# Norm gains applied at the transposes' eviction, a fifth slot for split weights, constants first, wider pauses in the compressed branch

## The reference

```python
def rms_norm(x, gain):
    y = x * lax.rsqrt(jnp.mean(x * x, axis=-1, keepdims=True) + NORM_EPS)
    return y * gain

# first block, for l in 0, 1
x = x + 0.5 * swiglu(rms_norm(x, ffn1_norm[l]), ...)        # 1024 -> 2816 -> 1024
x = x + hybrid_mixer(rms_norm(x, mix_norm[l]), ...)         # MLA, MoBA and dilated attention, gated
x = x + 0.5 * swiglu(rms_norm(x, ffn2_norm[l]), ...)
x = rms_norm(x, final_norm)
# second block, for l in 0, 1
h = rms_norm_2(x, norm_g[l])
x = x + concat(fox_attention(h), conformer_conv(h), nsa_attention(h)) @ w_out[l]
out = rms_norm_2(x, final_g)
```

## Time and profile before

| | |
|---|---|
| median of 3 runs | 1692.33 us |
| the profiled execution | 1691.58 us |
| its span | 1689.8 us |
| TensorE busy | 1630.5 us, 96% |
| VectorE busy | 960.7 us, 57% |
| ScalarE busy | 788.7 us, 47% |
| GpSimd busy | 149.9 us, 9% |
| loaded and stored | 273.76 MB, mean 162 GB/s |
| mean granted TensorE clock | 0.991 |

### The profile page before, as it was taken

How to read it: one execution, slowest core, us unless ns; L and a number is a source line. 1 busy time by engine, 2 the same in 40 slices (tenths; PEclk the granted TensorE clock), 3 DMA queues, 4 the chain that set the end, 5 groups by cost and what they waited for, 6 DMA issues and landing times. The chain is left out here.

```text
span 1689.8 us, 23056 instructions
## 1 busy us (share of the span) xinstructions
PE 1630.5 (96%) x8818; PEld 1378.0 (82%) x8818; DVE 960.7 (57%) x1399; ACT 788.7 (47%) x1246; POOL 149.9 (9%) x180
## 2 busy tenths in 40 slices
PE   7999999999999999999999999999999998999897
PEld 5888799877878887888889977778887777878686
DVE  4555564344665545555455444565554677767675
ACT  4444354445354444444355444554443444444443
POOL 0000012211200000000012111210000200010000
PEclk9999999999999999999999999999999999999999
DMA  7665455343455555655545443355655543244421
GB/s 255 206 205 197 156 192 167 131 131 113 156 186 183 191 183 166 202 193 177 181 159 186 139 134 111 131 188 192 202 187 162 174 147 132 69 160 143 150 94 50
DMA packets 77581, 273.76 MB, mean 162 GB/s; under 512 B 8608, under 2 KB 9632, under 8 KB 77472
## 3 DMA queue, kind: packets, MB, share of 16 engines
q1 hardware_dynamic: 77472, 272.30, 48.9%
HBM read 271.21 MB, written 1.05 MB: 161 GB/s over the span
## 5 line engine op out<-in xcount | busy, mean ns | idle before, releaser
L289 DVE TENSOR_TENSOR wlo<-raw,whi 128x1024 fp32r<-128x1024 f32 (+4 forms) x468 | 559.6, 1200 | 428.9 <-ACT whi L283 404.2
L283 ACT ACTIVATE whi<-raw 128x1024 fp32r<-128x1024 f32 (+3 forms) x496 | 510.0, 1032 | 474.2 <-PE bank L339 456.5
L337 PE MATMUL bank<-whi,hh 128*128 128x512 f32 (+4 forms) x1312 | 498.0, 380 | 9.9 <-DVE wlo L289 8.5
L339 PE MATMUL bank<-whi,hl 128*128 128x512 f32 (+4 forms) x1312 | 487.1, 371 | 0.0
L338 PE MATMUL bank<-wlo,hh 128*128 128x512 f32 (+4 forms) x1312 | 486.6, 371 | 0.0
L337 PEld LDWEIGHTS bank<-whi,hh 128*128 128x128 f32 x1312 | 248.6, 189 | 54.1 <-ACT whi L283 7.5
L339 PEld LDWEIGHTS bank<-whi,hl 128*128 128x128 f32 x1312 | 248.1, 189 | 40.4
L338 PEld LDWEIGHTS bank<-wlo,hh 128*128 128x128 f32 x1312 | 248.7, 190 | 36.0
L337 PE MATMUL bank<-hh,whi 128*128 128x256 f32 x480 | 145.2, 302 | 0.0
L339 PE MATMUL bank<-whi,gl 128*128 128x512 f32 x352 | 140.3, 399 | 0.0
L337 PE MATMUL bank<-whi,gh 128*128 128x512 f32 x352 | 138.8, 394 | 0.0
(11 more groups left out here) (288 smaller groups left out, 1743.0 us busy)
## 6 DMA issues: line engine op xcount, KB each, us to landing
raw<-W SPq DMA_DIRECT2D x464, 512.0 KB, 3.4
raw<-W SPq DMA_DIRECT2D x26, 384.0 KB, 3.6
gbc<-gains SPq DMA_DIRECT2D x10, 512.0 KB, 4.6
raw<-W SPq DMA_DIRECT2D x8, 416.0 KB, 3.0
tab<-tab SPq DMA_DIRECT2D x6, 384.0 KB, 3.9
raw<-W SPq DMA_DIRECT2D x4, 426.0 KB, 3.1
raw<-W SPq DMA_DIRECT2D x6, 192.0 KB, 3.1
x<-x_in SPq DMA_DIRECT2D x2, 512.0 KB, 5.6
```

The source lines that it names most:

```text
L283: high = act.op(lambda e: e.activation(whi[i][:, 0:w], r[:, 0:w], ACT.Copy), self.landed[c], free)
L289: tok = (low or dve).op(lambda e: e.tensor_tensor(wlo[i][:, 0:w], r[:, 0:w], whi[i][:, 0:w].bitcast(F), ALU.subtract), self.landed[c], hig ...
L337: pe.op(lambda e: e.matmul(dst, ah, bh, start=start, stop=False), *tokens, mark=False)
L339: return pe.op(lambda e: e.matmul(dst, al, bh, start=False, stop=stop), mark=mark)
```

## The change

It has four parts.

**Gains.** The gains no longer come as rows. For every norm but the two that need rows, the eight 128-column pieces of the gain are eight columns of `kc` (`K_GAIN`), made on the host. `first` does nothing; `turn` transposes x itself, and a bank is left by four scaled ScalarE copies (a column of the gain as scale) into `hh` and four VectorE scalar_tensor_tensor, bank * gain - hh, into `hl`. With two norms in a row, the product of both gains is the column, and the squares of x, x * first gain and the squares of that come behind the transposes (`squares`). The two gains needed as rows (for x itself there, and for the output) are loaded into a piece of `tab` early in the FFN before.

**Slots.** NSPLIT is 5, `held` stays 4 (`HELD`), and a chunk is prepared ahead only once its load is issued (`self.landed`).

**Start.** The constants are loaded first, then x; the two banks of t=0 alternate with the first two chunks' splits, and the squares follow.

**Compressed branch.** A `yield` moves ahead of the square, and the pauses behind it are 2, 2 and later 3 where they were 1, 1 and 2.

```diff
@@ -18,7 +18,8 @@
 FF_GROUPS = [(0, 512), (512, 512), (1024, 512), (1536, 512), (2048, 512), (2560, 256)]
 CH = 1024
 NRAW = 4
-NSPLIT = 4
+NSPLIT = 5
+HELD = 4
 WHOLE = ("cmp",)
 EPS = 1e-6
 BIG = 3e38
...
-                while self.split < min(len(widths), c + NSPLIT) and (
+                while self.split < c + NSPLIT and self.split in self.landed and (
                         self.split < NSPLIT or self.split - NSPLIT in self.done_tok):
                     self.prepare()
                 if c not in self.parts:
...
@@ -539,38 +529,43 @@
                 return stat[:, self.col(t) + 3:self.col(t) + 4]
 
             def first(self, t, h):
-                n, hs = self.n, slice(h * 512, (h + 1) * 512)
-                xs = x[:, t, hs]
+                self.row[t][h] = x_tok[t][h]
+
+            def turn(self, t, n):
+
+                i, bank, free = TB.take()
+                for k in range(4):
+                    src = x[:, t, (n * 4 + k) * 128:(n * 4 + k + 1) * 128]
+                    tok = tr(bank[:, k * 128:(k + 1) * 128], src, self.row[t][n], free, mark=(k == 3))
                 if self.gains == 2:
-                    ss = stat[:, self.col(t) + 4 + h:self.col(t) + 5 + h]
-                    a = a_fn(xn[:, t, hs], xs, ACT.Square, x_tok[t][h], Norm.xn_free[t], accum_out=ss)
-                    self.first_ms[t, h] = a
-                    x_tok[t][h] = tt(dve, xs, xs, gbc[n % 2][:, hs], ALU.mult, a, gain_tok[n])
-                    if t == 1 and h == 1:
-                        gain_free[n % 2] = x_tok[t][h]
-                    n += 1
-                self.row[t][h] = tt(dve, xn[:, t, hs], xs, gbc[n % 2][:, hs], ALU.mult, x_tok[t][h], gain_tok[n],
-                                    Norm.xn_free[t])
-                if t == 1 and h == 1:
-                    gain_free[n % 2] = self.row[t][h]
-
-            def second(self, t):
-                for n in range(2):
-                    i, bank, free = TB.take()
-                    for k in range(4):
-                        src = xn[:, t, (n * 4 + k) * 128:(n * 4 + k + 1) * 128]
-                        tok = tr(bank[:, k * 128:(k + 1) * 128], src, self.row[t][n], free, mark=(k == 3))
-                    hi = hh[:, n * 4:n * 4 + 4, t * 128:(t + 1) * 128]
-                    lo = hl[:, n * 4:n * 4 + 4, t * 128:(t + 1) * 128]
-                    _, low = parts_of(hi, lo, bank[:, :].rearrange("p (k n) -> p k n", k=4), tok)
-                    TB.give(i, low)
-                    self.ready[t, n] = low
-                Norm.xn_free[t], ss, v = mean_square(self.col(t), t, x, xn, x_tok[t], tok)
+                    g, g_tok = both_gains, both_tok
+                else:
+                    g, g_tok = kc[:, K_GAIN + self.n * 8:K_GAIN + (self.n + 1) * 8], kc_tok
+                each = [(bank[:, k * 128:(k + 1) * 128], g[:, n * 4 + k:n * 4 + k + 1],
+                         *(z[:, n * 4 + k, t * 128:(t + 1) * 128] for z in (hh, hl))) for k in range(4)]
+                for src, gk, hi, lo in each:
+                    high = a_scaled(hi, src, gk, tok, g_tok)
+                for src, gk, hi, lo in each:
+                    low = stt(lo, src, gk, hi.bitcast(F), ALU.mult, ALU.subtract, high, g_tok)
+                TB.give(i, low)
+                self.ready[t, n] = low
+                self.turned = tok
+
+            def squares(self, t):
+                if self.gains == 2:
+                    s1 = [stat[:, self.col(t) + 4 + h:self.col(t) + 5 + h] for h in range(2)]
+                    for h in range(2):
+                        hs = slice(h * 512, (h + 1) * 512)
+                        a1 = a_fn(xn[:, t, hs], x[:, t, hs], ACT.Square, x_tok[t][h], Norm.xn_free[t], accum_out=s1[h])
+                    for h in range(2):
+                        hs = slice(h * 512, (h + 1) * 512)
+                        x_tok[t][h] = tt(dve, x[:, t, hs], x[:, t, hs], tab[:, T2_GAIN + h * 512:T2_GAIN + (h + 1) * 512],
+                                         ALU.mult, a1, self.turned, tab_at[0])
+                Norm.xn_free[t], ss, v = mean_square(self.col(t), t, x, xn, x_tok[t], Norm.xn_free[t])
                 if self.gains == 1:
                     r = inverse_root(self.rs(t), ss, v)
                 else:
-                    s1 = [stat[:, self.col(t) + 4 + h:self.col(t) + 5 + h] for h in range(2)]
-                    b = tt(pool, s1[0], s1[0], s1[1], ALU.add, self.first_ms[t, 0], self.first_ms[t, 1])
+                    b = tt(pool, s1[0], s1[0], s1[1], ALU.add, a1)
                     r1 = inverse_root(s1[1], s1[0], b)
                     for _ in range(2):
                         v = tt(pool, ss, ss, s1[1], ALU.mult, v, r1)
...
 
                 i, src, tok = toks["hid"]
                 c = math.sqrt(2 / math.pi)
+                yield
                 e = a_fn(hidr[:, :, :], src, ACT.Square, tok, base)
-                yield
+                yield from pause(2)
                 d = ts(dve, hidr[:, :, :], hidr[:, :, :], 0.044715 * c, c, ALU.mult, ALU.add, e)
                 d = tt(dve, hidr[:, :, :], hidr[:, :, :], src, ALU.mult, d)
-                yield
+                yield from pause(2)
                 e = a_fn(hidr[:, :, :], hidr[:, :, :], ACT.Tanh, d)
                 yield from pause(2)
                 toks["gelu"] = stt(hidr[:, :, :], hidr[:, :, :], 1.0, src, ALU.add, ALU.mult, e)
                 M2.give(i, toks["gelu"])
-                yield from pause(2)
+                yield from pause(3)
                 i, bank, free = XB.take()
                 for kv in range(2):
                     for k in range(2):
...
 
         half_tok = pool.op(lambda e: e.memset(half[:, :], -0.5))
         mean_tok = pool.op(lambda e: e.memset(mean1[:, :], 1.0 / 256))
+        kc_tok = load(kc[:, :], cst, s_misc[3])
         x_tok = [[load(x[:, 0, :], x_in[0:128, :], s_misc[4])] * 2, None]
-        load_gain()
-        kc_tok = load(kc[:, :], cst, s_misc[3])
         st.fetch(2)
         x_tok[1] = [load(x[:, 1, :], x_in[128:256, :], s_misc[2])] * 2
         st.fetch()
-        load_gain()
         pool.wait(half_tok, mean_tok)
         pe.wait(kc_tok, mean_tok)
-        idr_tok = [a_copy(idr[:, :], ident, kc_tok),
-                   ts(dve, hide[:, :], causal[:, 128:256], -1.0, None, ALU.mult, None, kc_tok)]
+        both_gains = stat[:, 240:248]
+        both_tok = tt(pool, both_gains, *(kc[:, K_GAIN + n * 8:K_GAIN + (n + 1) * 8] for n in (6, 7)), ALU.mult, kc_tok)
 
         cur = Norm()
         for t in range(2):
             for h in range(2):
                 cur.first(t, h)
-            if t == 0:
-                cur.second(0)
-                st.prepare()
-                st.lows()
-                st.prepare()
-                st.lows()
-        load_gain()
+        for n in range(2):
+            cur.turn(0, n)
+            st.prepare()
+            st.lows()
+        cur.squares(0)
+        idr_tok = [a_copy(idr[:, :], ident, kc_tok),
+                   ts(dve, hide[:, :], causal[:, 128:256], -1.0, None, ALU.mult, None, kc_tok)]
 
         tab2_tok, tab_at = None, [None]
         for l in range(DEPTH):
...
```

45 lines of the change are left out of this document (20 added, 25 removed).

## The result

The changed kernel takes 1698.3 us (median of 10 runs, 1694.75 to 1698.94), the kernel before 1693.0 (10 runs, 1690.45 to 1694.46): a ratio of 1.0028, 95% interval 1.0018 to 1.0038. The forecast was 1688. The profiled execution took 1698.94 us with a span of 1697.1, 7.3 more than before. These two executions aren't the middle of their kernels: the profiled one of the changed kernel is the longest of its ten and that of before lies 1.4 us under the median, so 2 of the 7.3 us are in this choice.

A forecast was written before the change was run, and what follows sets the result against it. TensorE, busy 1630.5 of 1689.8 us, was taken as the bound, so only its waits and slow clock could be won. Terms -2.6 - 0.6 - 4.1 - 5.2 + 8 = -4.5 us gave 1688, range 1679 to 1698.

The forecast's parts named there:

- the compressed branch: Both layers: hidr wait goes, a ScalarE wait of some 2.2 us comes, one clock drop goes; -5.2 us (-14 to +1).
- the norm with two gains: Norm before the second block: old waits and clock drop go, new waits come; -4.1 us (-9.6 to +0.4).
- The end of the layers: End of each second-block layer: cw and oc transposes shift, qTh and qTl lie bare; +4 us a layer, +8 (+3 to +15).
- the first rival: Layer end: waits around the oc transposes drop the clock; 4.9 us a layer, 1698 in all; chance 0.15.
- the longer pauses and the fifth slot: Layer ends: the cause named for the order shifts costing +4 us a layer.
- the fifth slot: Elsewhere than the layer ends: 0 us (-2 to +2), as TensorE is never short of chunks inside a phase.
- I take one of the two drops of the clock as gone: Compressed branches: work now between the waits removes one of two half-clock drops, 3.4 us.
- the drop of the clock I take as gone: Norm before the second block: no two waits of 2 us follow each other any more, so 3.4 us are won.
- The start: Kernel start: transposes need less data and no product, first weight product about 10.2 for 13.79; -2.6 us (-3.6 to -1.5).
- the norms: Six ordinary norms: x*gain wait goes, eight copies delay ScalarE; 0.1 us gained each, -0.6 us (-5 to +4).
- the fourth rival: Eight copies put six norms 0.7 us behind each, two-gain norm keeps its drop; 9.1 us more, 1697; chance 0.07.

The follow-up runs named there:

- e1: Changed kernel with the compressed branch's old pauses (1, 1, 2, square first), gains, five slots and new start kept: 1688.6 us, ratio 0.997.
- e2: Changed kernel with four slots (NSPLIT 4), all else as changed: 1701.4 us, ratio 1.0059.
- e4: Kernel before with the change's new pauses alone: 1702.0 us, ratio 1.0059.
- e10: Changed kernel with its new pauses up to the hidr transposes, the next four pauses one turn shorter: 1690.7 us, ratio 0.9988.
- e6: Changed kernel with old pauses and, in the norm with two gains, the first root right behind the first squares: 1682.9 us, ratio 0.9946.
- e9: Kernel before with 16 unread small transposes ahead of the first mixer1: no run time given; lost clock at mixer1's ends 3.4 and 3.3 us.
- e14: Kernel before with 32 unread small transposes ahead of the first mixer1: no run time given; lost clock at mixer1's ends 3.0 (window cut) and 1.8 us.
- e15: Kernel before with 256 B per partition left free behind kc: 1689.8 us in a single run, down products 233.3 ns.
- e11: Kernel before with 288 B per partition left free behind kc: 1686.55 us, ratio 0.997, down products 228.9 ns.
- e16: Kernel before with 32 B per partition left free behind kc: 1687.1 us in a single run, down products 228.9 ns.
- e3: Changed kernel with old pauses and four slots, leaving only gains and new start: 1692.65 us, ratio 1.0000.

## Why the prediction was wrong

The forecast was 4.5 us faster, measured were 5.3 slower. The steps that failed are two gains that didn't come: a drop of the clock and a wait taken as gone in the compressed branch (7.5 us off by the marks), and a drop taken as gone with GpSimd's chain priced too low at the norm with two gains (6.0 off). The rest of the sum follows part by part.

**The end of the layers** (+8, measured +10.1, of which the sixth norm gives back some). The waits came as described: `cw` waits 1.23, `oc` 1.06, `qTl` 1.50. The half clock of the first rival came in part: behind the `oc` transposes only in the second layer (from 1675.7), with 1.7 us lost and not 3.4. In the first layer the clock is 1.00 there, and 1.7 us are lost 20 us earlier, behind the wait for `cw`. The cause was put wrongly: "the longer pauses and the fifth slot". e1, e2 and e4 show the pauses alone. VectorE's rows of the changed kernel show the two waits from the other side:

```profile
1484.68 2.35 DVE L289 TENSOR_TENSOR wlo<-raw,whi 128x1024 fp32r<-128x1024 f32 x2
...
1486.95 0.74 DVE L373 SCALAR_TENSOR_TENSOR oc<-oc,stat,rgn 128x512 f32<-128x512 f32 x1
...
1487.61 1.22 DVE L289 TENSOR_TENSOR wlo<-raw,whi 128x1024 fp32r<-128x1024 f32 x1
...
1489.07 0.69 DVE L365 TENSOR_TENSOR qTl<-bank,qTh 128x512 fp32r<-128x512 f32 x1 [0.24 <-ACT qTh L350]
```

The last `oc` product stands behind two low parts (2.35 us), as in e2, and `qTl` behind one, after which VectorE is idle for 0.24 us and waits for ScalarE's `qTh`: the 1.50 is the bare way from the transposes over ScalarE to VectorE. The low part ended 0.24 us before `qTh` was there, so without it the wait would be the same.

**The compressed branch** (-5.2, measured +2.3). The step that failed is "I take one of the two drops of the clock as gone", and with it that the waits would fall to 4.0: they are 6.6 in the first layer, with 0.6 for `kcl` gone behind them. The wait for `hidr` went, and the next link of the chain was late in its place (`kcv`, 1.25; in e10 4.59), beside two waits of 1.95 and 1.99 for ScalarE where one of some 2.2 was counted. The half clock still came in each layer, now behind `kcv`, with 3.4 us lost (windows 1427 and 1615). Setting the links further apart in the order didn't shorten the chain, it showed the wait elsewhere. What makes the chain itself long, small instructions queued behind splits of 1.2 us on VectorE for one, no run separated.

**The norm with two gains** (-4.1, measured +1.9). Failed: the price of GpSimd's chain. I took 1.6 us of wait; the rows of GpSimd are

```profile
1319.82 2.03 POOL L365 TENSOR_TENSOR stat<-stat 128x1 f32<-128x1 f32 x2
...
1321.94 1.05 POOL L370 TENSOR_SCALAR stat<-stat 128x1 f32<-128x1 f32 x1
...
1323.07 1.41 POOL L365 TENSOR_TENSOR stat<-stat,half 128x1 f32<-128x1 f32 x1
```

two products in 2.03, a scale and add in 1.05, a power in 1.41, where the same instructions of t=0 take 2.04, 0.19 and 0.55. Those of t=1 in the kernel before were faster:

```profile
1325.59 0.46 POOL L365 TENSOR_TENSOR stat<-stat 128x1 f32<-128x1 f32 x2
1326.13 0.19 POOL L370 TENSOR_SCALAR stat<-stat 128x1 f32<-128x1 f32 x1
1326.41 0.55 POOL L365 TENSOR_TENSOR stat<-stat,half 128x1 f32<-128x1 f32 x1
```

The slow ones run beside low parts on VectorE (1319.44 to 1324.07, and for the 2.04 of t=0 two from 1308.01), these fast ones beside none. No run takes the low parts away to test it. And failed again: "the drop of the clock I take as gone". Two came, with 1.7 and 3.4 us lost. With a shorter wait and neither drop e6 is 5.7 us faster than e1. Right were the prices of the copies: ScalarE's eight take 2.18 us (2.1 counted), VectorE's eight 2.16 (2.4 counted).

**Mixer1** (0, measured +2.8). Nothing in it was changed and its waits are the same to 0.02 us. At half clock were 3.4 us in each layer, and now are 6.8, so 1.7 us more are lost in each. e9, e14 and e15 (two, one or no stretch for the same waits) show that this is chance as far as the kernel's text goes, and the table compares one execution with one. The forecast had no term for it; a forecast for a program with such drops in it needs a margin of this size.

**The down phases** (0, measured -4.6, of which 4.2 is 240 products x 4.4 ns x 4). Wrong by a term that no view of waits shows. e11, e15 and e16 show that it is where the tensors behind `kc` lie, 32 B off the old place or not. This was luck: without it, by e11's 5.2 us, the change would be some 10 us slower than before.

**The start** (-2.6, measured -3.2) and **the norms** (-0.6, measured about -1.8 for five): right, the norms somewhat better than counted. What the fourth rival says of the norms, that the copies put each behind, was true of the gains alone (e3, where each of the six is 0.5 to 0.8 us later by the marks) and is hidden by the fifth slot (e1), which was costed at 0 and is worth 3 to 4 us.

The range's upper end, 1698, came from one rival at a time; measured were two terms of the wrong sign and a third unforeseen, held back by the down phases. That the time still came out within 0.3 us of that end is luck.

The Trainium skill, "TensorE: Matmul & The Clock Gate", Part 1, HAM oscillation, says of a kernel whose TensorE waits between bursts of products that it pays the change of the clock again at every burst. The traces agree in kind, with 22.2 us lost in that of the changed kernel; that the same waits pay not at all, once or twice is what e9, e14 and e15 add.

## What to carry to other kernels

Where small waits stand close together, look at the granted clock behind them in each trace before explaining a difference of a few us: here it was larger than the difference that was to be explained, and it changes from one execution to the next of the same kernel. So compare the mean granted clock of all runs as well, and don't take a difference of 2 or 3 us from one pair of traces. A pause put into one of several interleaved streams reorders all that comes behind it: give the turns back, or compare the order up to the program's end. When a change adds or removes a tensor, compare the start-to-start time of the products far from the edit; if it has moved, test the placement alone.

## What the runs showed that was not expected

- 32 B in the place of the tensors behind `kc` change a 128x512 product of the down phases from 233.3 to 228.9 ns (four placements: 0 and 256 B slow, 32 and 288 B fast), 1.9% of each product and 5 us of the kernel (e11). The products of gate and up take 226.6 to 226.9 ns in all of them (560 to 598 us).
- With the same three waits, no stretch at half clock (e15), one of 3.4 us or two, the last two in the two layers of one execution (e14).
- Executions of one kernel differ by 3 us with their mean granted clock (0.988 against 0.992).
- A GpSimd instruction on 128x1 takes 0.19 or 1.05 us (scale and add), 0.55 or 1.41 us (power).

What makes the placement matter inside the chip, and what made GpSimd's small instructions slow, was not separated further.
